# Choosing experts from stored scores and integer places, without the copies and casts between

## The reference, cut to what matters

```python
def peer_ffn(h, w_q, sub_keys, u, v):           # 8 heads, 128 keys per half, 16 picks, 16384 experts
    q = (xt @ w_q).reshape(T, PEER_HEADS, 2, PEER_HALF)
    sc = jnp.einsum('thcd,hckd->thck', q, sub_keys)
    s1, i1 = lax.top_k(sc[:, :, 0], K)          # K = 16
    s2, i2 = lax.top_k(sc[:, :, 1], K)
    cand = (s1[..., :, None] + s2[..., None, :]).reshape(T, PEER_HEADS, K * K)
    cand_idx = (i1[..., :, None] * NK + i2[..., None, :]).reshape(T, PEER_HEADS, K * K)
    top_s, top_pos = lax.top_k(cand, K)
    idx = jnp.take_along_axis(cand_idx, top_pos, axis=-1)
    gate = jax.nn.softmax(top_s, axis=-1)
    # per token: hid = gelu(u[idx] . x); out = sum over picks of gate * hid * v[idx]
```

## Time and profile before

| what | value |
|---|---|
| median of 3 runs | 2314.58 us (2314.29 to 2314.78) |
| the profiled execution | 2313.26 us, of which the span is 2311.5 us |
| busy share of the span | PE 90%, DVE 69%, ACT 48%, POOL 31% |
| moved by DMA | 726.73 MB, of which 539.00 MB on the gathers' queue |
| DMA engines | 55.5% of their span in the gathers' queue, 21.5% in SP's |

### The profile page before, as it was taken

One profiled execution on the slowest core, in us unless ns is written; L12 is line 12 of the kernel. 1 busy time (PEld: TensorE's weight loads), 2 busy tenths in 40 slices (PEclk: granted clock), 3 DMA queues, 4 the chain that ended last, 5 costly groups with the idle time before them and its releaser, 6 DMA issues.

```text
span 2311.5 us, 24618 instructions
## 1 busy us (share of the span) xinstructions
PE 2086.4 (90%) x8188; PEld 1331.3 (58%) x8188; DVE 1592.0 (69%) x3214; ACT 1104.6 (48%) x2463; POOL 711.0 (31%) x520
## 2 busy tenths in 40 slices
PE   8999999999989999997887889999899988788877
PEld 7888878889878545432322226988654532332224
DVE  7666666668866676767676766656676766767675
ACT  5335654346583444544544447345445444544446
POOL 0000000000100454565566640000354456465660
PEclk9999999999999999999999999999999999999999
DMA  7554425554426999999999995545999999999995
GB/s 276 183 194 169 146 92 190 193 185 152 147 100 264 393 427 427 427 427 427 426 427 427 427 413 215 213 146 224 367 423 427 427 426 427 427 427 427 427 427 211
DMA packets 101347, 726.73 MB, mean 314 GB/s; under 512 B 11632, under 2 KB 11888, under 8 KB 13424
## 3 DMA queue, kind: packets, MB, share of 16 engines
q0 software_dynamic: 74016, 539.00, 55.5%
q1 hardware_dynamic: 25200, 181.41, 21.5%
q10 hardware_dynamic: 2016, 4.89, 0.6%
HBM read 724.21 MB, written 1.05 MB: 314 GB/s over the span
## 4 chain that ended last, share of the span: by engine, by line
PE 27%; DMA 22%; DVE 10%; ACT 6%; issue 4%; POOL 4%; POOLq 0%; ACTq 0%; DVEq 0%
PE bank L2137 27%; DMA arena<-in_uv,expert 21%; DVE arena L2067 4%; POOL arena L778 3%; DMA gain<-in_uv,expert 2%; ACT L1266 1%; ACT L1226 1%; ACT w_hi L1273 1%; ACT arena L1270 1%; DVE sel_i L2014 1%; POOL wide L778 1%; DVE arena L2012 0%; ACT act_h L1266 0%; ACT w_hi_rounded L833 0%; DVE gain L2067 0%
## 5 line engine op out<-in xcount | busy, mean ns | idle before, releaser
L2137 PE MATMUL bank<-arena,w_hi 128*128 128x512 f32 x1736 | 843.7, 617 | 136.8 <-ACT w_hi L1273 135.1
L778 POOL DMA_INDIRECT arena<-in_uv,expert x434 | 589.1, 1357 | 787.1 <-DVE expert L1920 328.1
L2067 DVE SCALAR_TENSOR_TENSOR arena<-arena,xn 128x1024 f32<-128x1024 f32 x434 | 530.5, 1222 | 317.6 <-DMA arena<-in_uv,expert 306.6
L2137 PEld LDWEIGHTS bank<-arena,w_hi 128*128 128x128 f32 x1736 | 316.7, 193 | 596.3 <-ACT w_hi L1273 327.3
L833 ACT ACTIVATE w_hi_rounded<-lw 128x2048 fp32r<-128x2048 f32 (+1 forms) x159 | 286.2, 1810 | 296.6 <-PE bank L2137 275.4
L1378 DVE TENSOR_TENSOR lw_rounded<-lw,w_hi_rounded 128x2048 fp32r<-128x2048 f32 x139 | 320.6, 2308 | 124.8 <-ACT w_hi_rounded L833 124.1
L1266 ACT ACTIVATE act_h<-hid 128x1 f32<-128x1 f32 x512 | 103.5, 202 | 629.5 <-DVE arena L2067 527.5
L2137 PE MATMUL bank<-xT_rounded,w_hi_rounded 128*128 128x256 f32 (+2 forms) x1488 | 386.4, 337 | 6.6 <-DVE xT_rounded L1423 5.1
L2137 PE MATMUL bank<-xT_rounded,lw_rounded 128*128 128x256 f32 x1096 | 293.0, 280 | 0.0
L2137 PEld LDWEIGHTS bank<-xT_rounded,w_hi_rounded 128*128 128x128 f32 (+1 forms) x1488 | 248.8, 189 | 32.4 <-issue 5.8
L1273 ACT ACTIVATE w_hi<-consts,arena 128x128 f32<-128x128 f32 x512 | 205.6, 402 | 16.6
(11 more groups left out here) (276 smaller groups left out, 2122.6 us busy)
## 6 DMA issues: line engine op xcount, KB each, us to landing
lw<-in_units SPq DMA_DIRECT2D x159, 1024.0 KB, 4.7
arena<-in_uv,expert POOLq DMA_INDIRECT x434
arena<-in_units SPq DMA_DIRECT2D x6, 1024.0 KB, 9.1
wide<-in_wide POOLq DMA_DIRECT2D x2, 1024.0 KB, 8.9
gain<-in_gains ACTq DMA_DIRECT2D x4, 512.0 KB, 9.2
wide<-in_units SPq DMA_DIRECT2D x2, 1024.0 KB, 7.3
xT<-in_units SPq DMA_DIRECT2D x2, 1024.0 KB, 13.1
w_hi<-in_units SPq DMA_DIRECT2D x2, 1024.0 KB, 10.2
```

Of the source, the lines that this page charges most:

```text
L778: nc.gpsimd.indirect_dma_start(out=row_slot(slot), out_offset=None, in_=table, in_offset=bass.IndirectOffsetOnAxis(ap=expert[par][:, k:k + ...
L2067: V.scalar_tensor_tensor(row_slot(slot)[:, 0:D], row_slot(slot)[:, 0:D], 1.0, xn[:, tile, :], ALU.mult, ALU.mult, accum_out=hid[par][:, k: ...
L2137: return nc.tensor.matmul(o, lhsT, rhs, start=start, stop=stop, **more)
```

## The change

Three kinds of instruction go from the choice. In `pick`, the copy of a row's scores into `st` goes: the searches read `score` itself. In `pick` and `first_pick`, the casts of `top_i` to `top_f` and of `sel_ab` to `sel_f` go: the comparison and the product take the unsigned integers as they are, beside a float operand, with a float result. `first_pick` keeps its copy out of PSUM. With fewer instructions the counts that `pick` yields change, so its pieces fall between the dots in another way, and the number of counts in a row (`CHOICE`) goes from 25 to 22.

```diff
-                CHOICE = 25
+                CHOICE = 22
...
-                        link(V.tensor_copy(sel_f[:, :, at], sel_ab[:, :, at]))
                         for c in range(2):
-                            ins = V.tensor_tensor(hot[:, c, at, 0:n], sel_f[:, c, at].unsqueeze(2).to_broadcast(shape),
+                            ins = V.tensor_tensor(hot[:, c, at, 0:n], sel_ab[:, c, at].unsqueeze(2).to_broadcast(shape),
                                                   marks[:, c, 0:n].unsqueeze(1).to_broadcast(shape), ALU.is_equal)
...
-                                                  top_f[:, c, 0:n].unsqueeze(1).to_broadcast(shape), ALU.mult)
+                                                  top_i[:, c, 0:n].unsqueeze(1).to_broadcast(shape), ALU.mult)
...
-                    V.tensor_copy(top_f[:, :, early], top_i[:, :, early])
                     link(V.max_index(sel_p[:, early], sel_s[:, early], flat[0][:, 0:EARLY_ROWS * EARLY_ROWS]))
...
-                    V.tensor_copy(top_f[:, :, late], top_i[:, :, late])
...
-                    step(V.tensor_copy(st[:, 0], score[:, place_of(row), :].rearrange("p (c k) -> p c k", c=2)))
-                    yield 1
+                    scored = score[:, place_of(row), :].rearrange("p (c k) -> p c k", c=2)
                     for c in range(2):
-                        step(V.max(top_v[:, c, 0:8], st[:, 0, c]))
-                    yield 3
+                        step(V.max(top_v[:, c, 0:8], scored[:, c]))
+                    yield 2
                     for c in range(2):
-                        step(V.max_index(top_i[:, c, 0:8], top_v[:, c, 0:8], st[:, 0, c]))
+                        step(V.max_index(top_i[:, c, 0:8], top_v[:, c, 0:8], scored[:, c]))
...
-                    step(V.tensor_copy(top_f[:, :, :], top_i[:, :, :]))
...
-                    step(V.tensor_copy(sel_f[:, :, :], sel_ab[:, :, :]))
-                    yield 21
...
-                    step(V.tensor_tensor(hot[:, :, :, :], sel_f[:, :, :].unsqueeze(3).to_broadcast(each),
-                                         marks.unsqueeze(2).to_broadcast(each), ALU.is_equal))
-                    yield 22
-                    step(V.tensor_tensor(hot[:, :, :, :], hot[:, :, :, :], top_f[:, :, :].unsqueeze(2).to_broadcast(each), ALU.mult))
+                    step(V.tensor_tensor(hot[:, :, :, :], sel_ab[:, :, :].unsqueeze(3).to_broadcast(each),
+                                         marks.unsqueeze(2).to_broadcast(each), ALU.is_equal))
+                    yield 19
+                    step(V.tensor_tensor(hot[:, :, :, :], hot[:, :, :, :], top_i[:, :, :].unsqueeze(2).to_broadcast(each), ALU.mult))
```

More of the change, by code:

```diff
@@ L319, in build @@
         top_i = sb("top_i", [P, 2, TOPK], U32)
-        top_f = sb("top_f", [P, 2, TOPK])
         sel_s = sb("sel_s", [P, TOPK])
@@ L497, in build @@
         sel_ab = sb("sel_ab", [P, 2, TOPK], U32)
-        sel_f = sb("sel_f", [P, 2, TOPK])
         sel_i = sb("sel_i", [P, 2, TOPK])
@@ L1969, in pick @@
                     flat = [cand[:, i].rearrange("p a b -> p (a b)") for i in range(2)]
-                    step(V.tensor_copy(st[:, 0], score[:, place_of(row), :].rearrange("p (c k) -> p c k", c=2)))
-                    yield 1
+                    scored = score[:, place_of(row), :].rearrange("p (c k) -> p c k", c=2)
                     for c in range(2):
-                        step(V.max(top_v[:, c, 0:8], st[:, 0, c]))
-                    yield 3
+                        step(V.max(top_v[:, c, 0:8], scored[:, c]))
+                    yield 2
                     for c in range(2):
-                        step(V.max_index(top_i[:, c, 0:8], top_v[:, c, 0:8], st[:, 0, c]))
+                        step(V.max_index(top_i[:, c, 0:8], top_v[:, c, 0:8], scored[:, c]))
                     for c in range(2):
-                        step(V.match_replace(st[:, 1, c], top_v[:, c, 0:8], st[:, 0, c], LOWEST))
-                    yield 7
+                        step(V.match_replace(st[:, 1, c], top_v[:, c, 0:8], scored[:, c], LOWEST))
+                    yield 6
                     for c in range(2):
                         step(V.max(top_v[:, c, 8:], st[:, 1, c]))
-                    yield 9
+                    yield 8
                     step(sums(flat[0], TOPK))
@@ L1987, in pick @@
                         step(V.max_index(top_i[:, c, 8:], top_v[:, c, 8:], st[:, 1, c]))
+                    yield 11
+                    step(V.max(sel_s[:, 0:8], flat[0]))
                     yield 12
-                    step(V.max(sel_s[:, 0:8], flat[0]))
-                    yield 13
                     step(V.match_replace(flat[1], sel_s[:, 0:8], flat[0], LOWEST))
-                    step(V.tensor_copy(top_f[:, :, :], top_i[:, :, :]))
                     step(V.max_index(sel_p[:, 0:8], sel_s[:, 0:8], flat[0]))
-                    yield 16
+                    yield 14
@@ L1996, in pick @@
                     step(V.max(sel_s[:, 8:], flat[1]))
-                    yield 17
+                    yield 15
                     V.tensor_scalar(neg_top[:, :], sel_s[:, 0:1], -1.0, None, ALU.mult).then_inc(sel_ready, 1)
                     step(V.max_index(sel_p[:, 8:], sel_s[:, 8:], flat[1]))
-                    yield 18
+                    yield 16
                     step(V.tensor_scalar(sel_ab[:, 0, :], sel_p[:, :], 3, TOPK - 1, ALU.logical_shift_right, ALU.bitwise_and))
                     step(V.tensor_scalar(sel_ab[:, 1, :], sel_p[:, :], KEYS + EARLY_ROWS - 1, None, ALU.bitwise_and))
+                    yield 18
@@ L2004, in pick @@
+                    each = [P, 2, TOPK, TOPK]
+                    step(V.tensor_tensor(hot[:, :, :, :], sel_ab[:, :, :].unsqueeze(3).to_broadcast(each),
+                                         marks.unsqueeze(2).to_broadcast(each), ALU.is_equal))
+                    yield 19
+                    step(V.tensor_tensor(hot[:, :, :, :], hot[:, :, :, :], top_i[:, :, :].unsqueeze(2).to_broadcast(each), ALU.mult))
                     yield 20
-                    step(V.tensor_copy(sel_f[:, :, :], sel_ab[:, :, :]))
+                    step(V.tensor_reduce(sel_i[:, :, :], hot[:, :, :, :], AX_X, ALU.add))
@@ L2006, in pick @@
                     yield 21
-                    each = [P, 2, TOPK, TOPK]
-                    step(V.tensor_tensor(hot[:, :, :, :], sel_f[:, :, :].unsqueeze(3).to_broadcast(each),
-                                         marks.unsqueeze(2).to_broadcast(each), ALU.is_equal))
-                    yield 22
-                    step(V.tensor_tensor(hot[:, :, :, :], hot[:, :, :, :], top_f[:, :, :].unsqueeze(2).to_broadcast(each), ALU.mult))
-                    yield 23
-                    step(V.tensor_reduce(sel_i[:, :, :], hot[:, :, :, :], AX_X, ALU.add))
@@ L2015, in pick @@
-                    yield 24
                     V.scalar_tensor_tensor(expert[par][:, :], sel_i[:, 0, :], float(KEYS), sel_i[:, 1, :],
                                            ALU.mult, ALU.add).then_inc(expert_ready, 1)
-                    yield 24
+                    yield 21
                 def weigh(row, par):
```

## The result

The changed kernel takes 2330.31 us (median of 4 runs, 2329.29 to 2331.01); the kernel before takes 2314.68 in the same comparison. The ratio is 1.0064, with an interval of 1.0050 to 1.0078. So it is slower, by 15.6 us, where 2314.0 and no change were forecast; the range ended at 2315.9.

The account below looks back on a forecast made before the run. DMA, full in the lookups at 425 to 426 GB/s, was taken as the bound; only the first choice counted, 0.29 us a layer, so 2314.58 - 0.58 = 2314.0 us, with a range of 2311.7 to 2315.9.

Parts of the forecast that it names:

- What bounds the kernel: In the lookups, DMA is full at 426 GB/s: 256 gathers a layer take 630 us whatever DVE does.
- The parts of the change: Instructions removed, added and moved in the choices: 20.3 us of DVE in the rows costed at nothing, 0.58 us gained elsewhere.
- the rivals: Clock held in first layer 0.18, nothing arrives 0.12, clock falls in second 0.08, slower integers 0.05, DVE sets pace 0.02.
- the list of what would prove the forecast wrong: New 512-element times, PE waiting for row 0's fourth diagonal, or long stretches moving over 426 GB/s or becoming shorter.
- The first choice: Two casts leave the early half, on the chain ahead of PE's matmuls: 0.29 us saved a layer, 0.58 in two.
- The clock at the first start: Rival, chance 0.18: PE's clock holds in the first layer, its 16 matmuls take 1.63 us less, total 2312.4 us.
- the chosen forecast: Only the first choice's casts count, 0.58 us less in two layers: 2314.0 us, chance 0.55.
- Nothing from rows 1 to 15: A copy and two casts a row go, 20.3 us of DVE in all, worth nothing beside full DMA.
- Integer operands: Comparison and product of unsigned integers with floats on DVE take no longer; they stay near 0.69 us.
- The pieces between the dots: The gap between third and fourth dot grows from 0.73 to 1.57 us; costed at nothing.
- The fourth diagonal: The fourth dot's diagonal, ready at 768.61 instead of 767.77; PE takes it at 770.20, 1.59 us to spare.

Follow-up runs that it names:

- e1: The changed kernel plus an unused 128-byte tensor where top_f stood, restoring later tensors' old addresses; 2310.04 us, ratio 0.9989 to the kernel before.
- e3: The changed kernel plus 160 unused bytes where top_f stood, slots 32 bytes past a multiple of 256; 2333.42 us, ratio 1.0090 to the kernel before.
- e9: The changed kernel with slots back at multiples of 512, plus ten groups of plain loads after its last store; 427 to 422 GB/s at 8 KB.
- e2: The kernel before, instructions untouched, with top_f allocated behind the arena, so large tensors lie 128 bytes lower; 2330.16 us, ratio 1.0069 to the kernel before.
- e4: The changed kernel plus 64 unused bytes where top_f stood, slots 192 bytes past a multiple of 256; 2329.57 us, ratio 1.0071 to the kernel before.
- e7: The changed kernel with top_v allocated late, landing places at multiples of 256 but not of 512; 2310.65 us, ratio 0.9990 to the kernel before.
- e8: The changed kernel plus 96 unused bytes where top_f stood, slots 224 bytes past a multiple of 256; 2335.78 us, ratio 1.0099 to the kernel before.
- e6: The changed kernel with arena alone back at its old address, h to wide 128 bytes off; 2316.97 us, ratio 1.0014 to the kernel before.

## Why the prediction was wrong, point by point

- **What bounds the kernel: half right, and here it failed.** The failing step is "A gather is 1 MB, 1,048,576 bytes, so at 426 GB/s it takes 2.46 us, and 256 of them in each layer take 630 us whatever DVE does". DVE indeed doesn't matter. But the 426 GB/s of the kernel before was taken over for the kernel after without a reason, and it depends on addresses that the change moves. With 421 for 427 GB/s a gather takes 2.491 us for 2.456, and 512 of them 17.9 us more. Measured between the changed kernel and e1: the ratios 1.0064 / 0.9989 = 1.0075, or 17.4 us, and 19.7 us in the two lookups of the profiled executions.
- **The parts of the change: one was left out.** Instructions removed, added and moved were counted, and the deleted tensor was not. None of the rivals had the rate of the DMA engines in it, and the list of what would prove the forecast wrong names long stretches that move more, not less.
- **The first choice: right.** 0.29 us a layer was forecast from the cast rows; PE's gap shrank by 0.28 and 0.29.
- **The clock at the first start: the rival came true.** The 16 matmuls took 2.05 us for 3.68 in the changed kernel, as they do in e1 and in e3 to e9; in e2, with the old instructions, 3.23. A gap of 1.71 to 1.73 us was harmless in each of these nine; one of 2.00 or 2.01 was not, in the two kernels that had it. The rival forecast 2.2 us less than before. With the addresses held, e1 shows 0.0011 x 2313.62 = 2.5, by an interval of 0.5 to 4.6. That fits the rival better, but the interval holds the 0.58 of the chosen forecast as well, so it is the matmuls' rows that decide for the rival, and not the time.
- **Nothing from rows 1 to 15: right.** DVE's busy time fell from 1592.0 to 1576.4 us, by 15.6 where some 20 were forecast (why less was not worked out), and e1, whose addresses are the old ones, gained far less than 20.3.
- **Integer operands: right.** 692 ns for 693 in the comparison and 687 for 689 in the product.
- **The pieces between the dots: right.** The fourth diagonal was ready at 768.63 us (forecast 768.61), and PE took it at 770.20 as before. That these times agree so closely has some luck in it: the later start and the faster matmuls, 1.63 us each, cancel.
- **Open.** The first gather of the changed kernel starts 1.6 us later than before, and that lies ahead of the lookups. By kernel it starts at 748.26 (before), 749.89 (changed), 747.51 (e1), 750.02 (e2), 747.69 (e3), 748.12 (e4), 749.19 (e7), 747.31 (e8) and 752.38 (e9). Each is a single execution, and e1 and e9 have the same addresses, so no run ties it to the placement.

## What to carry to other kernels

Where DMA is full, ask of a change not only which bytes and instructions it moves but where the bytes land: deleting a small unused tensor can shift every later allocation. Hold the places where large transfers land at multiples of 256 bytes of a partition, by padding or by allocating them first. A share of 1.01 says that the engines are busy and not that they are at their best: compare the GB/s at the same share, and where an edit makes a kernel slower by the same amount everywhere, test the addresses with one line of padding before its logic.

## What the runs showed of the hardware

- Where all landing places start off a multiple of 256 bytes in SBUF, a piece costs a DMA engine 3.6 to 5.1 ns more on the average, at 1 to 8 KB 128 bytes off (e9) and, for the gathers' pieces of 8 KB, at each of the four distances tried (427 GB/s falls to 420 or 421). Where 15% of the gathers landed off the multiple (e6), no price showed: 427 GB/s. A start in HBM 128 bytes off costs nothing (428).
- A comparison and a product of an unsigned integer with a float take as long as of two floats on DVE: 692 and 687 ns for 512 elements, against 693 and 689.
